# Nine pairs of seven half-width products for the state-space input projection, with the residual parked in DRAM

## The reference

```python
glu_in, z, xbc, dt_raw, gate_in = jnp.split(n @ w_in, cuts, axis=-1)   # n: 512 tokens x 1024
xbc = jax.nn.silu(_causal_dwconv(xbc, ssm_conv_w, ssm_conv_b))         # 3072 channels, 4 taps
xs, bm, cm = jnp.split(xbc, [D_INNER, D_INNER + SSM_GROUPS * SSM_STATE], axis=-1)
dt = jax.nn.softplus(dt_raw.astype(f32) + dt_bias.astype(f32))
y = _ssd(xh, dt, a, ...)                                               # starts from x * dt
g_cv, g_ssm = jnp.split(jax.nn.sigmoid(gate_in), 2, axis=-1)
return (g_cv * y_cv + g_ssm * y_ssm) @ w_mix_out
h = h + g1 * _mixer(n1, ...)                                           # h is the residual
```

## Time and profile before

| what | value |
|---|---|
| median of 3 runs | 2986.26 us (2981.34 to 2986.8) |
| profiled execution | 2975.56 us, span 2973.5 us |
| granted TensorE clock, mean | 0.968 |
| TensorE busy | 2680.6 us (90%) |
| VectorE busy | 1822.5 us (61%) |
| ScalarE, GpSimd busy | 628.1 us, 635.2 us (21% each) |

### The profile page before, as it was taken

How to read it: one execution, slowest core, us unless ns; L and a number is a source line. 1 busy time by engine, 2 the same in 40 slices (tenths; PEclk the granted TensorE clock), 3 DMA queues, 4 the chain that set the end, 5 groups by cost and what they waited for, 6 DMA issues and landing times.

```text
span 2973.5 us, 54265 instructions
## 1 busy us (share of the span) xinstructions
PE 2680.6 (90%) x22266; PEld 1745.2 (59%) x22267; DVE 1822.5 (61%) x3266; ACT 628.1 (21%) x1262; POOL 635.2 (21%) x631
## 2 busy tenths in 40 slices
PE   7997999999999877777777778999899999998998
PEld 3444444577875544444444444766568877755687
DVE  4567599627658766666666667833564548246544
ACT  3118102101220000000000002313453113144420
POOL 2005102224430000000000004120264541204642
PEclk9999999999999999999999999999999999999999
DMA  8346222134259999999999995311003222200120
GB/s 237 123 159 247 87 74 85 57 114 167 67 226 398 428 428 428 429 428 429 428 429 428 429 428 215 120 66 57 1 1 114 85 86 102 85 29 1 45 98 29
DMA packets 118825, 586.40 MB, mean 197 GB/s; under 512 B 8900, under 2 KB 27940, under 8 KB 92980
## 3 DMA queue, kind: packets, MB, share of 16 engines
q1 hardware_dynamic: 116432, 583.20, 48.9%
q0 software_dynamic: 848, 1.21, 0.8%
q10 hardware_dynamic: 1428, 0.40, 0.1%
HBM read 581.95 MB, written 2.83 MB: 197 GB/s over the span
## 4 chain that ended last, share of the span: by engine, by line
PE 61%; DMA 28%; DVE 10%; issue 1%; ACT 1%; SPq 0%; DVEq 0%; ACTq 0%
PE PS L2233 27%; DMA S<-in_w 26%; PE PS L1971 24%; PE PS L1035 7%; DVE NTT L1710 1%; PE PS L1283 1%; DVE RSTD L1666 1%; DMA ring<-decay_rows 1%; DVE NTT L774 0%; DVE S L1753 0%; DVE PS L1849 0%; DVE NTT L2894 0%; DVE tri L2845 0%; DMA ring<-in_w_in 0%; DVE S L3020 0%
## 5 line engine op out<-in xcount | busy, mean ns | idle before, releaser
L2233 PE MATMUL PS<-NTT,ring 128*128 128x512 f32 x1248 | 548.0, 596 | 6.1 <-DMA ring<-in_w_in 2.6
L2233 PEld LDWEIGHTS PS<-NTT,ring 128*128 128x128 f32 x1248 | 235.0, 191 | 292.0 <-issue 279.7
L675 DVE SCALAR_TENSOR_TENSOR xT<-PS,MOD,xT 128x512 f32<-128x512 f32 x520 | 354.3, 744 | 20.0 <-PE PS L2233 20.0
L2233 PE MATMUL PS<-S,SQ 128*32 128x128 f32 (+1 forms) x4352 | 204.5, 342 | 93.1 <-DMA S<-in_w 91.0
L2233 PE MATMUL PS<-NTT,SQ 128*32 128x128 f32 (+1 forms) x4800 | 225.3, 338 | 33.6 <-DMA NTT<-in_w 28.6
L2233 PEld LDWEIGHTS PS<-S,SQ 128*32 128x32 f32 x4352 | 128.7, 117 | 187.6 <-DMA S<-in_w 133.5
L1971 PE MATMUL PS<-NTT,ring 128*128 128x256 f32 x928 | 224.9, 388 | 11.8 <-ACT PAIR L2018 9.5
L2233 PEld LDWEIGHTS PS<-NTT,SQ 128*32 128x32 f32 x4800 | 150.5, 117 | 115.9 <-DMA NTT<-in_w 41.0
L961 POOL TENSOR_SCALAR NTT<-xT,AD 128x512 f32<-128x512 f32 x4 | 6.5, 1634 | 941.0 <-DVE xT L675 941.0
L2233 PE MATMUL PS<-NTT,LS 32*128 32x512 f32 (+1 forms) x1060 | 204.4, 621 | 1.7 <-DVE xT L675 1.2
L1971 PEld LDWEIGHTS PS<-NTT,ring 128*128 128x128 f32 x928 | 178.9, 194 | 44.9 <-ACT PAIR L2018 9.4
(11 more groups left out here) (468 smaller groups left out, 4041.0 us busy)
## 6 DMA issues: line engine op xcount, KB each, us to landing
S<-in_w SPq DMA_DIRECT2D x87, 2048.0 KB, 40.9
ring<-in_w SPq DMA_DIRECT2D x63, 2048.0 KB, 41.2
NTT<-in_w SPq DMA_DIRECT2D x42, 2048.0 KB, 41.2
ring<-in_w_in SPq DMA_DIRECT2D x40, 2048.0 KB, 7.8
ring<-in_w_ada SPq DMA_DIRECT2D x12, 2048.0 KB, 11.1
NTT<-decay_rows SPq DMA_DIRECT2D x20, 640.0 KB, 5.5
ring<-in_w_ssm_out SPq DMA_DIRECT2D x4, 2048.0 KB, 8.3
ring<-in_cmp_w SPq DMA_DIRECT2D x4, 2048.0 KB, 8.4
```

Source lines behind the costliest of these rows:

```text
L675: return dve.scalar_tensor_tensor(out=xT[:, k, :], in0=PS[:, bank, :], scalar=MOD[:, 40 + k:41 + k], in1=xT[:, k, :], op0=ALU.mult, op1=AL ...
L2233: return pe.matmul(o, l, r, start=start, stop=stop)
```

## The change

Of the 24 chunks, the first four (SINGLE = 4) and the last two (CLOSING = 2) stay as they are on TensorE. The 18 between are made as nine pairs of seven products. The four sums of weight blocks go to one set of places (`one_set_sums`: `SQ`, `RSTD` and a block of the slab itself), so that the first of the next pair waits for the second product and the others for the sixth. The column sums of `nT` move from behind the scan to behind chunk 2, into the place of `xT`; for that SyncE stores `xT` to DRAM first (`residual_d`) and loads it again after mix pair 2. The unshifted tap is no longer done by VectorE: ScalarE makes it as a second, scaled copy of the bank (`xbc_copy`). `xdt` is called one chunk sooner.

```diff
+        def one_set_sums(pool, n, blocks, s_):
+            (a11, a12), (a21, a22) = blocks
+            if n:
+                pool.wait_ge(S("fp"), 7 * (n - 1) + 2)
+            pool.tensor_tensor(s_[0], a21, a22, ALU.add).then_inc(S("matrix_sum"), 1)
+            pool.wait_ge(S("matrix_sum"), 4 * n + 1)
+            if n:
+                pool.wait_ge(S("fp"), 7 * (n - 1) + 6)
...
+                if i == XBC_AT[1] + 1:
+                    sp.wait_ge(S("norm_scaled"), AFTER["n1_scaled"] + KD)
+                    sp.wait_ge(S("square_used"), KD)
+                    sp.dma_start(residual_d, xT_[:, :]).then_inc(S("x_landed"), 16)
+                if i == CO_AT[4]:
+                    sp.wait_ge(S("x_landed"), 32)
+                    sp.wait_ge(S("fp"), 7 * (MIX0 + 3))
+                    sp.dma_start(xT_[:, :], residual_d).then_inc(S("x_landed"), 16)
...
+            cumulative_sums()
+            pe.wait_ge(S("scalar_milestone"), AFTER["cums_copied"] + 2)
+            for q in range(XBCP):
+                c0 = SINGLE + 2 * q
+                blocks, s_ = xbc_pair(q)
+                landed(pe, XBC_AT[c0 // 4])
+                seven_products(pe, q, xbc_bank(c0), xbc_bank(c0 + 1), XBC_Z, blocks, s_, 4, nT, fourth(TS), sum_counts(0),
+                               (S("xbc_evac"), 2 * (c0 if q < 2 else c0 - 2)), (None, 0))
+                for c in (c0, c0 + 1):
+                    if 5 <= c < 5 + KI:
+                        xs_turn(c - 5)
+                    if c in ADA_COLUMNS_AT:
+                        later_columns(ADA_COLUMNS_AT[c])
...
+            def xbc_copy(c):
+                if c >= 3:
+                    act.wait_ge(S("xbc_conv"), c - 2)
+                act.activation(XP[:, c % 3, SSM_K - 1:SSM_K - 1 + T], PS[:, xbc_bank(c), :], ACT.Copy) \
+                    .then_inc(S("xbc_evac"), 1)
+                if c >= 2:
+                    act.wait_ge(S("xbc_done"), c - 1)
+                act.activation(CA[:, c % 2, :], PS[:, xbc_bank(c), :], ACT.Copy,
+                               scale=COL[:, C_SCW + KX * (SSM_K - 1) + c:C_SCW + KX * (SSM_K - 1) + c + 1]) \
+                    .then_inc(S("xbc_evac"), 1)
...
+            act.wait_ge(S("rr_stored"), 16)
+            for q in range(XBCP):
+                c = SINGLE + 2 * q
+                pair_first_copy(act, q, xbc_bank(c))
+                if q:
+                    xbc_silu(c - 2)
+                pair_second_copy(act, q, xbc_bank(c + 1), XBC57)
+                xbc_silu(c - 1)
+                for e in range(2):
+                    act.wait_ge(S("combined"), 2 * q + e + 1)
+                    xbc_copy(c + e)
...
+            for q in range(XBCP):
+                c0 = SINGLE + 2 * q
+                pair_combine(dve, link, q, xbc_bank(c0), xbc_bank(c0 + 1), XBC_Z, XBC57, XBCU)
+                for c in (c0, c0 + 1):
+                    if 5 <= c <= 20:
+                        ada_product(2 * (c - 5))
+                        ada_product(2 * (c - 5) + 1)
+                    xbc_taps(c)
+                    if 5 <= c < 5 + KI:
+                        xdt(c - 5)
...
-            dve.wait_ge(S("fp"), 7 * SSMP)
-            first_sums(CVT, nT)
-            right_sums(0, CVT, nT, 0, 2)
-            right_sums(0, CVT, nT, 2, 5)
+            dve.wait_ge(S("fp"), 7 * MIX0)
```

More of the change, by code:

```diff
@@ L202, in build, with xbc_pair, xbc_bank @@
         SSM57, SSMU = v3(SQ_[:, 0:512], 256), v3(SQ_[:, 512:1024], 256)
+        TS = xT_[:, :].rearrange("p (q k t) -> p q k t", q=4, k=4)
+        XBC57, XBCU = v3(TAIL[:, 10496:11008], 256), v3(TAIL[:, 7180:7692], 256)
+        XBC_BANKS, XBC_Z = ((5, 6), (7, 3)), 4
+        residual_d = nc.dram_tensor("residual", [P, KD * T], F32).ap()
+        def xbc_pair(q):
+            c = SINGLE + 2 * q
+            w, c0 = v3(slot(XBC_AT[c // 4]), 512), P * (c % 4)
+            blocks = [[w[:, 4 * h:4 * h + 4, c0 + P * n:c0 + P * n + P] for h in range(2)] for n in range(2)]
+            return blocks, (v3(SQ_[:, 0:512], P), v3(SQ_[:, 512:1024], P), blocks[1][0], v3(RSTD[:, :], P))
+        def xbc_bank(c):
+            return 5 + c % 3 if c < SINGLE else XBC_BANKS[(c - SINGLE) // 2 % 2][c % 2]
         SSM_BANKS = ((4, 5, 6), (7, 0, 1))
@@ L2129, in _, with xbc_sums @@
             pool.dma_start(tables_d[1], PANG[:, 0:NA]).then_inc(S("pos_landed"), 16)
+            def xbc_sums(q):
+                blocks, s_ = xbc_pair(q)
+                if q == 0:
+                    pool.wait_ge(S("square_used"), KD)
+                    pool.wait_ge(S("rstd_used"), 1)
+                landed(pool, XBC_AT[(SINGLE + 2 * q) // 4])
+                one_set_sums(pool, q, blocks, s_)
+            xbc_sums(0)
             pool.wait_ge(S("scalar_milestone"), AFTER["cums_copied"] + 2)
             pool.dma_start(rr_d, RR[0:HEADS, :]).then_inc(S("rr_stored"), 16)
+            for q in range(1, XBCP):
+                xbc_sums(q)
             pool.wait_ge(S("small_landed"), 176)
+            pool.wait_ge(S("combined"), 2 * XBCP)
             def skip_matrix(c):
@@ L2361, in group_cb @@
+            for c in range(KX - CLOSING, KX):
+                pe.wait_ge(S("xbc_evac"), 2 * (KX - 2 * CLOSING))
+                xbc_product(c)
             def group_cb(g):
@@ L2848, in _, with right_sums, first_sums, xbc_taps @@
             dve.wait_ge(S("conv_pad"), 3)
-            for c in range(KX):
+            def right_sums(base, to, B, k0, steps):
+                for q in (2, 1, 3):
+                    if q == 1:
+                        dve.wait_ge(S("dve_sum"), base + 2)
+                    if q == 3:
+                        dve.wait_ge(S("dve_sum"), base + steps + 2)
+                    column_sum(dve, q, tuple(to[:, r] for r in range(4)), B, 4, k0, k0 + 2).then_inc(S("dve_sum"), 1)
+            def first_sums(to, B):
+                for k0 in (0, 2):
+                    column_sum(dve, 0, tuple(to[:, r] for r in range(4)), B, 4, k0, k0 + 2).then_inc(S("dve_sum"), 1)
+            def xbc_taps(c):
+                dve.wait_ge(S("xbc_evac"), 2 * c + 2)
+                for k in range(SSM_K - 1):
+                    w_ = COL[:, C_SCW + KX * k + c:C_SCW + KX * k + c + 1]
+                    i_ = dve.scalar_tensor_tensor(out=CA[:, c % 2, :], in0=XP[:, c % 3, k:k + T], scalar=w_,
+                                                  in1=CA[:, c % 2, :], op0=ALU.mult, op1=ALU.add)
+                    if k < SSM_K - 2:
+                        link(i_)
+                    else:
+                        i_.then_inc(S("xbc_conv"), 1)
+            for c in range(SINGLE):
                 if c == 1:
```

254 lines of the change are left out of this document (119 added, 135 removed).

## The result

The changed kernel takes 3009.7 us (median of 5 runs, 3001.0 to 3014.3), the kernel before beside it 2986.3 us (5 runs). The ratio is 1.0079, 95% interval 1.0055 to 1.0104: slower, by 0.8%. The forecast was 3008 us, in a range of 2993 to 3018. The profiled execution has a span of 2999.2 us, 25.7 us more than before.

What follows compares the result with a forecast made beforehand. TensorE was taken to bound the state-space input stage without a break. Arithmetic saved 15.0 us, but new waits, clock and small terms brought the sum to +21.8 us: 2986.3 + 21.8 = 3008.1 us, 80% range 2993 to 3018.

Steps and rivals of the forecast that it cites:

- 1 arithmetic: State-space input on TensorE: nine seven-product pairs save 1.66 us each against two single chunks, -15.0 us.
- 2 start of pair 0: Pair 0's third product waits for the decay rows' store behind tables and weight sums on GpSimd's queue: +10.7 us.
- 3 before pair 1: Pair 1 waits until VectorE's combination and ScalarE's two copies clear pair 0 from PSUM: +3.2 us.
- 4 behind even pairs: Behind pairs 2, 4, 6 and 8, TensorE's modulation columns wait for VectorE's steps behind the combination: +14.8 us.
- 5 clock: After TensorE's waits its granted clock falls to 0.50: five times 2.0 us, +10 us, bounds 2 to 14 us.
- 6 last chunk; mix: ScalarE's second copy lengthens the last chunk's path, +0.1 us; column sums leaving the path ahead of the convolution's mean, -2.0 us.
- the forecast without the hold: If GpSimd's sums did not slow VectorE's operations: 1.6 us before pair 1, 7 us behind pairs 2, 4, 6 and 8.
- its +4 us: Exclusive port lock for whole instructions would add about 1 us per late pair, some 4 us in sum; the forecast left it out.
- rival A: TensorE's clock stays granted except at the start, clock loss 2 us instead of 10: +13.8 us, 3000 us; chance 0.26.
- B: VectorE and GpSimd do not hold one another up; short waits leave the clock alone: +4.3 us, 2990.6 us; chance 0.14.
- C: TensorE runs all nine pairs at its own pace, VectorE's steps done before the turns end: -6.3 us, 2980 us; chance 0.05.
- D: More waits than seen, such as a late slab or the residual's store: +30 us, 3016 us; chance 0.09.

Runs made afterwards that it cites:

- the last kernel: Changed kernel with GpSimd's start reordered (weight sums, decay-row store, tables), first chunk's modulation steps ahead of the combination, pair 1 awaiting chunks 0 to 3 alone: 2976.1 us, ratio 0.9968.
- column sums again: Changed kernel with the residual's eight column-sum additions made a second time after the gate and read by the first mix products: 3013.5 us (one run).
- small sums: Changed kernel with GpSimd's weight sums of pairs 1 to 8 and the gate pairs on one column instead of 512: stage 162.9 us against 176.3.
- the filler: Changed kernel with seven unread products on TensorE ahead of each of four waits for VectorE's modulation step, behind pairs 2, 4, 6, 8: 2999.0 us.

## Why the prediction was right

By its own items, in us:

| item | forecast | measured | from |
|---|---|---|---|
| 1 arithmetic | -15.0 | -14.8 | stage 139.4 of the last kernel less 152.6, less the wait of 1.6 |
| 2 start of pair 0 | +10.7 | +8.0 | waits of 1.58, 2.42, 4.04 |
| 3 before pair 1 | +3.2 | +3.0 | wait |
| 4 behind even pairs | +14.8 | +11.0 | waits 3.03, 3.03, 3.04, 1.86 |
| 5 clock | +10 | +16.5 | 36.9 less the waits of 6.5, 3.0 and 11.0; by place 3.7, 1.7 and 10.9 |
| 6 last chunk; mix | +0.1; -2.0 | 0; -2.0 | column sums again |
| sum | +21.8 | +21.7 | stage +23.7, mix -2.0 |

The measured column adds up to the stage because item 5 is what is left of it; the places counted one by one (3.7 at the start, 1.7 behind pair 1's wait, 10.9 behind the four column waits) make 16.3. That the two sums agree is luck: I had item 4 3.8 us and item 2 2.7 us too high, and item 5 6.5 us too low. The places, the engines that release them and the direction were all as forecast.

**Item 1** holds. A pair takes 12.09 us (121.88 to 133.97 in the changed kernel) as in the mix.

**Item 2** had the right chain, GpSimd's queue, and missed two things. I let the first product start with the end of the cumulative sums; it waits 1.58 us for ScalarE, since a pair opens PSUM that the sums occupy. I could have seen that: the wait stands in the diff behind `cumulative_sums()`, and ScalarE's copy ends at 83.6, 1.6 us after the sums. And the store landed in 2.3 us, not in 3.6, which is the row of before. Counted from the end of the sums the third product came after 12.6 us, where I forecast 14.2. Of these 12.6 us, 8.0 are waits, 3.5 the two products at full clock and 1.1 their slow clock, which the table has under item 5. The wait of 6.2 us that item 5 gives to this place follows only if the second product waits for the first weight sum; item 2 doesn't say so, but that is what happened, in waits of 2.42 and 4.04 us.

**Items 3 and 4.** The combination takes 3.74 us at odd pairs and 3.2 at even ones; I had 4.0. At odd pairs each held operation loses 0.6 to 0.7 us, not 0.8. At even pairs the combination starts 0.5 us late, not 1.0, because VectorE comes from its taps and `xdt` without a pause, and by then the sum at L2040 is more than half done, so it holds L2062 for only 0.2 us. What I left out is the steps: the sum at L2043 holds them too (1.82 instead of 1.53 us). The unheld combination and steps alone would still leave waits of 1.43 us (small sums), near the 1.6 us of the forecast without the hold.

How the hold works, seen at pair 1, VectorE first, then GpSimd:

```profile
120.00 1.14 DVE L2062 TENSOR_TENSOR NTT<-NTT 128x256 f32<-128x256 f32 x1
...
121.52 1.04 DVE L2064 TENSOR_TENSOR NTT<-NTT 128x256 f32<-128x256 f32 x1
...
119.59 1.27 POOL L2040 TENSOR_TENSOR SQ<-SQ,ring 128x512 f32<-128x512 f32 x1 [5.64 <-PE PS L1989]
120.94 1.33 POOL L2042 TENSOR_TENSOR RSTD<-ring,SQ 128x512 f32<-128x512 f32 x1
```

L2062 ends at 121.14, 0.28 us after GpSimd's sum (120.86), and L2064 at 122.56, 0.29 us after the next (122.27), where each takes 0.42 us alone: most of its work starts only when the other is done. The Trainium skill, page SBUF — State Buffer, section "SBUF: two separate sides", says the port pair is held exclusively for the whole instruction; for these short operations the trace nearly agrees (1.14 and 1.04 us measured, 1.28 and 1.17 by the rule). For the steps beside sums it agrees less: in the kernel with the sums behind the combination, two steps and the sum among them would take 2.80 us one after the other (1.53 + 1.27, from rows where each runs alone); the steps were done in 2.41 us, and the sum, which took 1.64 us, ran from 136.13 to 137.77 inside them. The rule was off by 0.13 to 0.14 us a held operation and 0.4 us there, so refusing its +4 us was right.

**Item 5** is the term that failed in size. I had 2.0 us for each of five waits. All six places cost, between 1.7 and 3.7 us each, and with the small sums even waits of 1.43 us cost 2.0 us. Behind the waits that rival A calls "only a little longer than 3 us" the clock fell every time.

**The rivals.** A (clock granted throughout, 3000) fell with the windows and with the filler. B (no hold, 2990.6) fell with the durations of 1.03 to 1.14 us; its world, made by the small sums, still lost clock behind three of its five short waits. C (faster, 2980) needed both steps within 2.6 us of the sixth product. The changed kernel doesn't have that, but a change of order in one place does: with the steps first, they no longer stand behind the combination at all. I had named the condition and judged it closed, since the combination alone takes 2.42 us; I had not seen that the order of the two was free. D (late slab, residual's store) did not occur: the residual's store landed in 31.2 us, at 76.8, and held VectorE's first column sum by 5.2 us off the path. A slab did come late for GpSimd (its first sum for pair 4 waited for one until 147.42), but TensorE needed that sum at 157.06.

Open: what decides whether the clock falls and for how long. Behind the same wait of 3.03 us in the same place it cost 2.0 us in some executions and 3.6 in others, so neither the place nor the wait explains it; and it fell behind 1.43 us but not behind 1.58, 1.72 and, once, 1.87 us. No run here separates that.

## What to carry to other kernels

When one engine's work is moved behind another step of the same engine, ask which of the two the bound engine waits for, and put that first; here two instructions in the wrong place cost 21.8 us and hid all of an arithmetic gain of 14.8. Price a wait of the bound TensorE as the wait plus what its clock takes afterwards: here 16.5 us on top of 20.4 us of waits. And follow a DMA's issue through its queue: the order of two table stores, four weight sums and one store on GpSimd cost 10.1 us.

## What the hardware showed that I had not expected

- The clock fell behind a wait of 1.43 us with a group of short turns ahead of it (1.04 us) and 128x1 products behind it: about 3.5 us at 0.50, 2.0 us lost. I had not counted a wait under 3 us as one that costs clock. In the same trace it stayed at 1.00 behind 1.72 us ahead of pair 1, with 128x256 products behind, and behind 1.87 us after pair 8.
- What one wait of 3.03 us costs in clock differs from trace to trace with the same code at that place: 2.0 or 3.6 us behind pair 2.
- Filling a wait of 3.03 us with products that nobody reads kept the clock at 1.00 and saved 8.8 us over four waits.
- VectorE and GpSimd held each other up in both orders tried: sums taken away from a combination (3.2 to 2.4 us) lengthened the steps by 0.6 us (1.82 to 2.41) and the first of them itself from 1.27 to 1.64 us.
- Unchanged stages scatter between executions by 11 us (2161.2 to 2172.4 us from the router on), about half of the change's effect. Whether part of that hangs on the kernel isn't shown, since each kernel has one trace. A stage between two landmarks shows more than the whole time.
